# One layer of three attention groups on one core: how the rotary part of group B's scores is multiplied, and the order in which the out-projection begins

## The chip, the cores and the metric

The kernel runs on one core of a Trainium2 chip. The metric is the device time of one execution in microseconds (us), the median of several executions. TensorE (PE, with its weight loads PEld) multiplies; VectorE (DVE), ScalarE (ACT) and GpSimd (POOL) work beside it; SyncE (SP) and POOL issue the transfers.

## The reference

The layer computes, for 1024 tokens of width 2048 in float32:

```
h = RMSNorm(x);  proj = h @ W_in            # split among the groups
group A: 16 heads, 2 key heads, width 64, windows of 128 keys, sinks
group B: 4 heads; score = (q_nope . k_nope + q_rope . k_rope) * 192**-0.5
         q_nope 128 wide, q_rope 64 wide, k_rope shared by the heads
         mask: key chunk <= query chunk (chunks of 64); softmax; times v
group M: 4 heads of 128 over 256 memory tokens
y = x + [silu(gA)*A | silu(gB)*B | silu(gM)*M] @ W_o
```

`q_rope` and `k_rope` are RMS-normalised and rotated by the position. The output is y, 1024 x 2048.

## The kernel before

All stages use all five engines, each with its own instruction list written out by hand and semaphores between them. In order of time:

1. **In-projection** (to about 806 us). Weights stream from memory in chunks of 128x1024. Every float32 product is made of three fp32r matmuls (`three`, L1535): both operands are split into a high part (fp32r) and a low part (the rest), and hi\*hi, hi\*lo and lo\*hi are added in PSUM. ACT makes the high parts (`high`, L604), DVE the low ones (`low`, L935).
2. **Memory keys and values** (806 to 858 us, loop at L1607), in the same way. Beside it DVE normalises and rotates B's rotary key (`kr_d`, L1193 to L1198) and writes it twice side by side; TensorE transposes it (L1638), ACT keeps rows 0 to 63 in `krT[:, 0]` and rows 64 to 127 in `krT[:, 1]` (L744). The other half of each is zero (DVE, L1202). So a 128-row product with two heads' stacked queries picks one head.
3. **Up-projection of group B** (858 to about 940 us), eight token tiles. The step of a tile on TensorE is `up_in` (six transposes into PSUM banks 0 and 1), `up` (24 matmuls for queries, then 12 for keys and values) and `up_back` (transposes of the finished queries and keys of the tile two before: 2 rotary, 4+4 others). DVE squares, normalises and rotates (`up_squares`, `up_norm`), and makes the low part of the next tile's input (`up_in`, L1206). ACT keeps what is transposed (`up_keep`).
4. **Group A** (to about 1005 us), **group B** (to 1126 us) and **group M** (to 1165 us). Each is a pipeline of steps: scores on TensorE, maximum on DVE, exponent on ACT, normalisation on DVE, transposes on TensorE (`turn_p`), copy on ACT (`keep_pT`), values on TensorE, gating on DVE. On TensorE step s of group B is score(s+2), value(s-1), turn_p(s). A step is one head and one tile of 128 queries against 128 to 1024 keys; there are 32. A score of group B is, per 512 keys, one float32 matmul for the 128-wide part (L1719) and one for the rotary part (L1720). In the profile a float32 matmul is two instructions.
5. **Out-projection** (1165 us to the end): eight visits (pairs of output tiles) of eight units. Units 0 to 3 are the left half of the contraction in a seven-product scheme (Strassen-Winograd, products P1 to P7, 21 matmuls of 128x512), units 4 to 7 are plain (24 matmuls). The order within a visit is 0 to 7. In visit 0 ACT and DVE also split the gated attention results into high and low parts, unit by unit (`left_sums`, `left_high`, `left_low`, `plain_high`, `plain_low`), some of it beside group M (`ahead`). The weights of a unit come through three buffers `z` (SP), with sums by DVE (`z_make`), high part by ACT (`z_high`), low part by DVE (`z_low`). POOL loads x into `xq` and stores y from it.

The gates of the groups come by POOL's transfers into `mixed` (L562, L567, L572), which the gating multiplies in place. The probabilities of group B (`b_p`) lie at the start of the region of the raw weights.

Of the kernel before, what the change touches and what calls it, by code (L numbers as in the profile page):

```python
# [29 lines left out]
P = 128  # L30
# [40 lines left out]
NOUT = NVISIT * NUNIT  # L71
ZRING, HRING = 3, 2
# [54 lines left out]
def layer(nc, io):  # L127
    with ExitStack() as ctx:
# [46 lines left out]
        kr_d = at("kr_d", [P, TT, 2, BR], F32, R0 + 41984)  # L175
# [12 lines left out]
        qrT = at("qrT", [P, BH // 2, SEQ], F32, R0 + 49152)  # L188
        krT = at("krT", [P, 2, SEQ], F32, R0 + 57344)
# [47 lines left out]
        c_lo = put("c_lo", [P, 2, 6, P], F32R)  # L237
        u_tmp = at("u_tmp", [P, 2, 4, 32], F32, RS + 14336)
# [14 lines left out]
        b_p = at("b_p", [P, 2, SEQ], F32, WRAW)  # L253
# [13 lines left out]
        plain_at = [RT + 8192, RT + 12288] + [RS + 4096 * k for k in range(6)]  # L267
# [4 lines left out]
        zh_at = (R0 + 61440, small_at + 3584)  # L272
        z_hi = [at(f"z_hi{i}", [P, 7, P], F32R, zh_at[i]) for i in range(HRING)]
        xq = at("xq", [P, 4, HALF], F32, small_at + 7168)
        part_a = at("part_a", [P, HALF], F32, small_at + 15360)
        part_b = at("part_b", [P, HALF], F32, small_at + 17408)
        assert small_at + 19456 <= nc.sbuf_usable_end
# [61 lines left out]
        kn_loaded, kn_turned, kn_kept, zeroed = sem("kn_loaded"), sem("kn_turned"), sem("kn_kept"), sem("zeroed")  # L339
# [25 lines left out]
        def blocks_to(c):  # L365

            return NBLOCK * (c // NUNIT) + min(c % NUNIT, NBLOCK - 1) + 1

        def rotary_place(t):

            return (2, slice(0, 256)) if t < TT - 3 else (1, slice(256 * (t % 2), 256 * (t % 2) + 256))
# [3 lines left out]
        def _(sp):  # L375
# [83 lines left out]
            def load_z(c):  # L459
                wait(sp, z_used, c - ZRING + 1)  # L460
                if c % ZRING == 2:
                    sp.wait_ge(M.gated, TT)
                sp.dma_start(z[c % ZRING][:, 0:4, :], io["w_out"][c]).then_inc(z_loaded[c % ZRING], 16)
# [5 lines left out]
            for c in range(2, NOUT):  # L469
                load_z(c)  # L470


        @block.gpsimd
        def _(pool):
# [93 lines left out]
            for i in range(TT // 2):  # L568
# [3 lines left out]
                pool.dma_start(mixed[:, AJ + BH:KT, tok], gate_s[AJ + BH:KT, :, tok].rearrange("j p s -> p j s")  # L572
                               ).then_inc(M.gates_loaded, 16)

            def quad(a, visit, q):

                return a[2 * visit + q % 2, :, q // 2 * HALF:(q // 2 + 1) * HALF]

            pool.wait_ge(M.gated, TT)
            for visit in range(NVISIT + 1):  # L580
                for q in range(4):
                    if visit >= 1:
# [1391 lines left out]
```

## Time and profile before

| | us |
|---|---|
| median of 3 runs | 1513.98 (1510.68 to 1514.11) |
| the profiled execution, its own time | 1507.98 |
| its span | 1506.2 |
| PE busy | 1464.1 (97% of the span) |
| DVE busy | 671.9 (45%) |
| ACT busy | 469.2 (31%) |
| PE's share of the chain that ended last | 90% |

The granted clock of TensorE was 0.997 of full speed on average. The profile's first part gives the busy time of each engine; the chain of waits gives what each part of the end hung on. Because PE is busy nearly throughout, what counts is PE's own time, and in the few stretches where it idles, whom it waits for.

### The profile page before, as it was taken

Reading aid. Unit: us, or ns where it says so; the run is one execution under the profiler, and the core shown is the slowest. Engines: PE = TensorE matmul, PEld = TensorE weight load, DVE = VectorE, ACT = ScalarE, POOL = GpSimd, SP = SyncE. Lnnn points to the kernel's source line nnn. Section 1 sums busy time; section 2 is a strip of 40 time slices with the busy share of each in tenths; the row PEclk is TensorE's granted clock in tenths of the full one; section 3 lists DMA queues with packets and bytes.
Section 4 is the critical chain, followed back from the end, with each engine's and each line's share of the span. In section 5 each row is a group of like instructions: output and inputs, shape, how many; then the busy total and the mean of one; then the engine's idle time right before and its main releaser. Section 6 shows DMA issues by size and latency. Waiting matters only on the chain.

```text
span 1506.2 us, 17987 instructions
## 1 busy us (share of the span) xinstructions
PE 1464.1 (97%) x7118; PEld 1195.7 (79%) x7118; DVE 671.9 (45%) x1055; ACT 469.2 (31%) x842; POOL 130.6 (9%) x141
## 2 busy tenths in 40 slices
PE   9999999999999999999999998889998999999997
PEld 7888888888888888887887787656777788888886
DVE  4332241442614131312226767975659654444542
ACT  4551301313131020201234456974456411111110
POOL 1010000202001000000001022100000011111110
PEclk9999999999999999999999999999999999999999
DMA  9541231121123121221444521540020233333331
GB/s 359 196 107 56 98 111 55 42 101 52 42 102 108 57 97 56 81 72 43 167 154 155 181 84 42 155 127 15 15 71 17 75 112 106 105 112 105 108 109 49
DMA packets 48812, 146.78 MB, mean 97 GB/s; under 512 B 5616, under 2 KB 9712, under 8 KB 47472
## 3 DMA queue, kind: packets, MB, share of 16 engines
q1 hardware_dynamic: 33136, 84.42, 17.8%
q0 software_dynamic: 15472, 61.51, 11.7%
q8 instruction: 41, 0.67, 0.2%
q14 instruction: 19, 0.16, 0.0%
q10 hardware_dynamic: 144, 0.02, 0.0%
HBM read 117.61 MB, written 28.32 MB: 97 GB/s over the span
## 4 chain that ended last, share of the span: by engine, by line
PE 90%; ACT 5%; DVE 3%; issue 1%; DMA 0%; POOL 0%; ACTq 0%; SPq 0%; DVEq 0%
PE ps L1537 26%; PE ps L1539 26%; PE ps L1538 26%; ACT a_p L805 3%; PE ps L1756 2%; PE ps L1719 2%; PE ps L1720 2%; PE ps L1737 1%; PE ps L1723 1%; PE ps L1762 1%; PE ps L1591 0%; PE ps L1590 0%; DVE w_lo L938 0%; ACT st L803 0%; PE ps L1741 0%
## 5 line engine op out<-in xcount | busy, mean ns | idle before, releaser
L938 DVE TENSOR_TENSOR w_lo<-w_raw,w_hi 128x1024 fp32r<-128x1024 f32 x87 | 106.6, 1225 | 504.0 <-ACT w_hi L608 503.6
L608 ACT ACTIVATE w_hi<-w_raw 128x1024 fp32r<-128x1024 f32 x89 | 94.2, 1059 | 593.8 <-PE ps L1539 573.9
L1537 PE MATMUL ps<-w_hi,h_hi 128*128 128x512 f32 x640 | 249.5, 390 | 1.4 <-DVE h_lo L953 1.4
L1539 PE MATMUL ps<-w_hi,h_lo 128*128 128x512 f32 x640 | 249.4, 390 | 0.0
L1538 PE MATMUL ps<-w_lo,h_hi 128*128 128x512 f32 x640 | 249.3, 390 | 0.0
L1539 PE MATMUL ps<-h_hi,w_lo 128*128 128x512 f32 x512 | 199.5, 390 | 0.0
L1537 PE MATMUL ps<-h_hi,w_hi 128*128 128x512 f32 x512 | 199.5, 390 | 0.0
L1538 PE MATMUL ps<-h_lo,w_hi 128*128 128x512 f32 x512 | 199.5, 390 | 0.0
L1538 PE MATMUL ps<-mixed_lo,z_hi 128*128 128x512 f32 x384 | 149.6, 390 | 0.0
L1537 PEld LDWEIGHTS ps<-w_hi,h_hi 128*128 128x128 f32 x640 | 120.2, 188 | 26.5 <-issue 1.6
L1539 PEld LDWEIGHTS ps<-w_hi,h_lo 128*128 128x128 f32 x640 | 120.2, 188 | 24.9
L1538 PEld LDWEIGHTS ps<-w_lo,h_hi 128*128 128x128 f32 x640 | 120.2, 188 | 24.9
L883 ACT ACTIVATE z_hi<-z 128x896 fp32r<-128x896 f32 (+1 forms) x64 | 50.7, 792 | 255.3 <-PE ps L1539 203.4
L1430 DVE TENSOR_TENSOR z_lo<-z,z_hi 128x896 fp32r<-128x896 f32 (+1 forms) x64 | 57.1, 892 | 130.6 <-ACT z_hi L883 130.6
L1537 PEld LDWEIGHTS ps<-h_hi,w_hi 128*128 128x128 f32 x512 | 96.1, 188 | 20.1
L1539 PEld LDWEIGHTS ps<-h_hi,w_lo 128*128 128x128 f32 x512 | 96.1, 188 | 19.9
L1538 PEld LDWEIGHTS ps<-h_lo,w_hi 128*128 128x128 f32 x512 | 96.1, 188 | 19.8
L1539 PE MATMUL ps<-plain_hi,z_lo 128*128 128x512 f32 x256 | 99.7, 390 | 0.0
L1537 PE MATMUL ps<-plain_hi,z_hi 128*128 128x512 f32 x256 | 99.7, 390 | 0.0
L1537 PE MATMUL ps<-left_hi,z_hi 128*128 128x512 f32 x224 | 87.6, 391 | 4.2 <-DVE left_slo L1407 2.1
L1539 PE MATMUL ps<-left_hi,z_lo 128*128 128x512 f32 x224 | 87.3, 390 | 0.0
L1538 PEld LDWEIGHTS ps<-mixed_lo,z_hi 128*128 128x128 f32 x384 | 72.1, 188 | 14.9
(270 smaller groups left out, 2090.9 us busy)
## 6 DMA issues: line engine op xcount, KB each, us to landing
w_raw<-in_w SPq DMA_DIRECT2D x89, 512.0 KB, 3.5
z<-in_w_out SPq DMA_DIRECT2D x64, 256.0 KB, 2.7
x_nat<-in_x POOLq DMA_DIRECT2D x8, 1024.0 KB, 8.6
mixed<-gate_s POOLq DMA_DIRECT2D x16, 512.0 KB, 4.9
xq<-in_xT POOLq DMA_DIRECT2D x32, 256.0 KB, 4.5
out_y<-xq POOLq DMA_DIRECT2D x32, 256.0 KB, 2.6
x_raw<-in_xT SPq DMA_DIRECT2D x7, 1024.0 KB, 18.2
gate_s<-T POOLq DMA_DIRECT2D x3, 2048.0 KB, 7.0
```

Of the source, the lines that this page charges most:

```text
L608: a.activation(w_hi[:, n % SPLIT, :], w_raw[:, n % RAW, :], ACT.Copy).then_inc(hi_ready, 1)
L805: ins = a.activation(a_p[:, par, e, :], ps[:, 2 + 2 * par + e // 4, e % 4 * P:(e % 4 + 1) * P], ACT.Exp, bias=st[:, par, 1, e:e + 1], scal ...
L883: a.activation(flat(z_hi[c % HRING][:, 0:n, :]), flat(z[c % ZRING][:, 0:n, :]), ACT.Copy).then_inc(z_hi_made, 1)
L938: v.tensor_tensor(w_lo[:, n % SPLIT, :], w_raw[:, n % RAW, :], w_hi[:, n % SPLIT, :].bitcast(F32), ALU.subtract).then_inc(lo_ready, 1)
L1430: v.tensor_tensor(flat(z_lo[c % ZRING][:, 0:n, :]), flat(z[c % ZRING][:, 0:n, :]), flat(z_hi[c % HRING][:, 0:n, :]).bitcast(F32), ALU.subt ...
L1537: mm(out, a_hi, b_hi, start=start, stop=False)
L1538: mm(out, a_hi, b_lo, start=False, stop=False)
L1539: return mm(out, a_lo, b_hi, start=False, stop=stop)
L1719: mm(out, qnT[:, h, q], knT[:, h, a:b], start=True, stop=False)
L1720: ins = mm(out, qrT[:, h // 2, q], krT[:, h % 2, a:b], start=False, stop=True)
L1723: ins = mm(ps[:, bank + h // 2, h % 2 * NMEM:(h % 2 + 1) * NMEM], c_qT[:, par, h, :], kmT[:, h, :], start=True, stop=True)
L1756: ins = mm(ps[:, 1, 0:P], vB[:, k, h * BV:(h + 1) * BV], b_pT[:, par, k * P:(k + 1) * P], start=(k == 0), stop=(k == t))
```

## The change

Rotary part of group B:

- The rotary query of a head is stored stacked: 64 rows of high part (fp32r) over 64 rows of low part, instead of two heads stacked in float32. DVE makes both after the rotation (`u_r`, two more operations in a tile). There are four 128-column transposes of a tile for it in place of two, in two groups: heads 0 and 1 where the two transposes stood, heads 2 and 3 between the two halves of `up` two tiles later (for the first five tiles), and in `up_back` for the last three. The second group waits until DVE has made the low part of the next tile's input, because both use PSUM bank 1. ACT copies each group by itself.
- The rotary key is kept twice: `kr_high` is high over high, `kr_low` is low over zero. With the stacked query, the first product gives (q_hi + q_lo) * k_hi and the second q_hi * k_lo. 16 transposes in place of 8; the two clearing operations on `krT` go, one smaller one comes.
- A score is then two fp32r matmuls (at least 256 keys wide, so some columns are computed and not used) and one float32 matmul.
- `b_p` moves into the rows of `mixed` that hold the gates of M's heads 0 and 1, so these gates are loaded only after B's last transpose, by one transfer of 1 MB, for which M's gating waits (`late_gates`).

Out-projection:

- The units of a visit go in the order 0, 1, 4, 2, 5, 3, 6, 7, and the weights are loaded in that order.
- The products P1, P5 and P7, P2 and P3 of the first unit are issued between the last steps of group M, P4 before M's last gating, and only P6 waits for it.
- The work beside M is laid out anew: weights of units 0 and 1 are finished there, the left operand of unit 2 later. Sums that leave PSUM are taken at unit positions 6 and 7 of every visit.
- Loads of x and stores of y move from POOL to SP, behind the weight loads of positions 2, 3 and 4.

```diff
+ORDER = (0, 1, 4, 2, 5, 3, 6, 7)
-        b_p = at("b_p", [P, 2, SEQ], F32, WRAW)
+        b_p = at("b_p", [P, 2, SEQ], F32, R1 + 49152)
@@ SP
+            def load_xq(visit):
+                for q in range(4):
+                    wait(sp, xq_moved[q], 32 * visit)
+                    sp.dma_start(xq[:, q, :], quad(io["xT"], visit, q)).then_inc(xq_moved[q], 16)
+            def store_y(visit):
+                for q in range(4):
+                    sp.wait_ge(drained, 9 * visit + 6 + q)
+                    sp.dma_start(quad(io["yT"], visit, q), xq[:, q, :]).then_inc(xq_moved[q], 16)
...
             for c in range(2, NOUT):
                 load_z(c)
+                if c == 2:
+                    load_xq(0)
+                if c >= NUNIT and c % NUNIT == 3:
+                    store_y(c // NUNIT - 1)
+                if c >= NUNIT and c % NUNIT == 4:
+                    load_xq(c // NUNIT)
@@ POOL
+            pool.wait_ge(B.p_turned, len(BSTEPS))
+            pool.dma_start(mixed[:, AJ + BH:AJ + BH + 2, :], gate_s[...]).then_inc(late_gates, 16)
@@ ACT
+            def keep_qr(t, i, bank, col):
+                act.wait_ge(u_qr, 2 * t + 2 - i)
+                a.activation(qr[i][:, :, t * P:(t + 1) * P],
+                             ps[:, bank, col:col + 256].rearrange("p (h s) -> p h s", h=2), ACT.Copy).then_inc(u_qr_kept, 1)
...
-                if 2 <= c <= 5:
-                    left_high(1 + (c - 2) // 2, c % 2)
-                if c == 6:
-                    z_high(0)
+                if c in (2, 3):
+                    left_high(1, c - 2)
+                if c in (4, 5):
+                    z_high(c - 4)
+                if c in (6, 7):
+                    left_high(2, c - 6)
+                    plain_high(c + 2)
@@ DVE
-            v.tensor_copy(kr_d[:, :, 1:2, :], kr_d[:, :, 0:1, :]).then_inc(kr_norm, 1)
+            steps.did(v.memset(kr_l0[:, :, 1, :].bitcast(F32), 0.0))
+            steps.did(v.tensor_copy(kr_hh[:, :, 0, :], kr_d[:, :, 0, :]))
+            do(v.tensor_copy(kr_hh[:, :, 1, :], kr_d[:, :, 0, :]))
+            v.tensor_tensor(kr_l0[:, :, 0, :], kr_d[:, :, 0, :], kr_hh[:, :, 0, :].bitcast(F32), ALU.subtract).then_inc(kr_norm, 1)
             low(n + 1)
-            for g in range(2):
-                rows = slice(64 - 64 * g, 128 - 64 * g)
-                v.memset(krT[rows, g, :], 0.0).then_inc(zeroed, 1)
...
-                v.tensor_tensor(d2, d2, u_tmp[:, 1], ALU.add).then_inc(u_done, 1)
+                do(v.tensor_tensor(d2, d2, u_tmp[:, 1], ALU.add))
+                do(v.tensor_copy(u_r[:, t % 2, :, 0, :], rope(u_fin)))
+                v.tensor_tensor(u_r[:, t % 2, :, 1, :], rope(u_fin), u_r[:, t % 2, :, 0, :].bitcast(F32), ALU.subtract
+                                ).then_inc(u_done, 1)
...
+                if at_ is M:
+                    dve.wait_ge(late_gates, 16)
...
+                if c in (0, 1):
+                    left_sums(1, c)
+                if c in (2, 3):
+                    z_make(c - 2)
+                if c in (5, 6):
+                    z_low(c - 5)
+                if c in (4, 5):
+                    left_sums(2, c - 4)
+                if c in (6, 7):
+                    left_low(1, c - 6)
@@ PE
+                if 0 <= t - 2 < SPLIT_TILES:            # in up(t), between queries and keys
+                    turn_qr(t - 2, 1, 1, 256)
...
+            def turn_qr(t, i, bank, col):
+                pe.wait_ge(u_done, t + 1)
+                if i == 1:
+                    pe.wait_ge(u_clo, min(t + 4, TT))
+                for h in range(2 * i, 2 * i + 2):
+                    ins = turn(ps[:, bank, col + (h - 2 * i) * P:col + (h - 2 * i + 1) * P],
+                               u_r[:, t % 2, h].rearrange("p a d -> p (a d)").bitcast(F32), ident[:])
+                if t < SPLIT_TILES or i == 1:
+                    ins.then_inc(u_qr, 1)
...
-                        mm(out, qnT[:, h, q], knT[:, h, a:b], start=True, stop=False)
-                        ins = mm(out, qrT[:, h // 2, q], krT[:, h % 2, a:b], start=False, stop=True)
+                        wide = max(b, a + 256)
+                        for kr, start in ((kr_high, True), (kr_low, False)):
+                            mm(ps[:, bank + a // HALF, 0:wide - a], qr[h // 2][:, h % 2, q], kr[:, a:wide], start=start, stop=False)
+                        ins = mm(out, qnT[:, h, q], knT[:, h, a:b], start=False, stop=True)
...
+            def out_begun(part):
+                if part == 0:
+                    pe.wait_ge(z_lo_made, 1)
+                    pe.wait_ge(left_lo_made, 2)
+                    pe.wait_ge(M.qT, TT)
+                    product(0, P1)
+                elif part == 1:
+                    pe.wait_ge(M.exp, TT)
+                    product(0, P5)
+                    product(0, P7)
+                else:
+                    product(0, P2)
+                    product(0, P3)
```

## Rows read from the trace of the kernel before

**Rows 1.** The page, part 1: busy time, share of the span, instructions.

```profile
PE 1464.1 (97%) x7118; PEld 1195.7 (79%) x7118; DVE 671.9 (45%) x1055; ACT 469.2 (31%) x842; POOL 130.6 (9%) x141
```

**Rows 2.** Stretches: length, busy PE, PEld, DVE, ACT, POOL, PEclk, DMA share, GB/s.

```profile
857.00:925.00 68.00, 67.79 (x398) 59.10 (x397) 43.96 (x97) 34.94 (x50) 16.60 (x8) 1.00 0.22 66
925.00:998.00 73.00, 60.04 (x585) 44.27 (x583) 65.56 (x142) 69.08 (x294) 10.44 (x11) 0.98 0.52 143
1060.00:1111.00 51.00, 50.41 (x269) 35.57 (x269) 28.62 (x88) 19.24 (x43) 1.51 (x2) 1.00 0.06 22
1126.00:1165.00 39.00, 33.39 (x250) 30.66 (x249) 35.63 (x50) 28.04 (x65) 0.00 (x0) 1.00 0.10 33
1165.00:1205.00 40.00, 35.85 (x155) 29.06 (x156) 27.56 (x39) 16.51 (x18) 2.15 (x4) 1.00 0.25 73
```

**Rows 3.** Timeline of PE in group B: start, length, instruction.

```profile
1101.58 0.60 PE L1720 MATMUL ps<-krT,qrT 128*128 128x256 f32 x2
1102.01 0.83 PE L1756 MATMUL ps<-b_pT,vB 128*128 128x128 f32 x6
...
1103.12 1.02 PE L1719 MATMUL ps<-knT,qnT 128*128 128x512 f32 x2
1103.98 1.02 PE L1720 MATMUL ps<-krT,qrT 128*128 128x512 f32 x2
```

**Rows 4.** Timeline of PE in the up-projection: fp32r matmuls of 512 and 256 columns.

```profile
869.56 0.39 PE L1539 MATMUL ps<-uq_hi,c_lo 128*128 128x512 f32 x1
869.79 0.28 PE L1537 MATMUL ps<-uq_hi,c_hi 128*128 128x256 f32 x1
869.90 0.28 PE L1538 MATMUL ps<-uq_lo,c_hi 128*128 128x256 f32 x1
```

**Rows 5.** Timeline of group B where one head ends and the next begins.

```profile
1085.15 1.60 PE L1756 MATMUL ps<-b_pT,vB 128*128 128x128 f32 x12 [0.45 <-ACT b_pT L824]
...
1087.55 0.92 ACT L824 ACTIVATE b_pT<-ps 128x896 f32<-128x896 f32 x1 [1.36 <-PE ps L1737]
...
1088.52 1.83 PE L1756 MATMUL ps<-b_pT,vB 128*128 128x128 f32 x14
```

**Rows 6.** Timeline of the up-projection, one tile: transposes, DVE's low part, key matmuls.

```profile
881.54 0.38 PE L1674 MATMUL ps<-ident,u_fin 128*128 128x128 f32 x2
881.76 0.60 PE L1678 MATMUL ps<-ident,u_fin 128*128 128x128 f32 x4
...
887.39 0.95 DVE L1206 TENSOR_TENSOR c_lo<-ps,c_hi 128x768 fp32r<-128x768 f32 x1
...
887.52 0.40 PE L1537 MATMUL ps<-ukv_hi,c_hi 128*128 128x512 f32 x1
```

**Rows 7.** Timeline of the memory stage: a clearing operation, and PE's longest wait.

```profile
834.82 0.91 DVE L1202 MEMSET krT<- 64x1024 f32 x1 [0.27 <-PE ps L1539]
...
839.70 0.50 PE L1537 MATMUL ps<-w_hi,m_hi 128*128 128x512 f32 x1 [2.07 <-DVE w_lo L938]
```

**Rows 8.** Timeline at the start of group A: the last tile's rotary query.

```profile
938.38 0.44 PE L1674 MATMUL ps<-ident,u_fin 128*128 128x128 f32 x2 [2.19 <-DVE u_fin L1268]
...
938.86 0.38 ACT L772 ACTIVATE qrT<-ps 128x256 f32<-128x256 f32 x1
```

**Rows 9.** Timeline of group M and the first matmul of the out-projection.

```profile
1122.23 0.75 POOL L572 DMA_DIRECT2D mixed<-gate_s  x1 [30.26 <-DVE mixed L1305]
...
1131.06 0.69 DVE L1305 TENSOR_TENSOR mixed<-ps,mixed 128x512 f32<-128x512 f32 x1 [0.40 <-PE ps L1762]
...
1165.74 0.50 PE L1537 MATMUL ps<-left_hi,z_hi 128*128 128x512 f32 x1 [0.78 <-DVE mixed L1305]
```

**Rows 10.** DMA issues: what, queue, count, KB each, median us to landing.

```profile
z<-in_w_out SPq DMA_DIRECT2D x64, 256.0 KB, 2.7
x_nat<-in_x POOLq DMA_DIRECT2D x8, 1024.0 KB, 8.6
mixed<-gate_s POOLq DMA_DIRECT2D x16, 512.0 KB, 4.9
xq<-in_xT POOLq DMA_DIRECT2D x32, 256.0 KB, 4.5
out_y<-xq POOLq DMA_DIRECT2D x32, 256.0 KB, 2.6
```

More of the change, by code:

```diff
@@ L365, in blocks_to, with unit, qr_steps @@
         def blocks_to(c):
-            return NBLOCK * (c // NUNIT) + min(c % NUNIT, NBLOCK - 1) + 1
-        def rotary_place(t):
-            return (2, slice(0, 256)) if t < TT - 3 else (1, slice(256 * (t % 2), 256 * (t % 2) + 256))
+            return NBLOCK * (c // NUNIT) + sum(u < NBLOCK for u in ORDER[:c % NUNIT + 1])
+        def unit(c):
+            return ORDER[c % NUNIT]
+        SPLIT_TILES = TT - 3
+        def qr_steps(t):
+            return t + min(t, SPLIT_TILES)
         @block.sync
@@ L470, in _ @@
                 load_z(c)
+                if c == 2:
[4 more added lines that the diff above has]
+                    load_xq(c // NUNIT)
+            store_y(NVISIT - 1)
+            for q in range(4):
+                sp.wait_ge(xq_moved[q], 32 * NVISIT)
         @block.gpsimd
@@ L1663, in up @@
                 ins.then_inc(u_up, 1)
+            def turn_qr(t, i, bank, col):
[7 more added lines that the diff above has]
+                    ins.then_inc(u_qr, 1)
             def up_back(t):
-                bank, cols = rotary_place(t)
-                rotary = ps[:, bank, cols]
                 fin = u_fin[:, t % 2]
-                pe.wait_ge(u_done, t + 1)
-                wait(pe, u_qr_kept, t)
+                wait(pe, u_qr_kept, qr_steps(t))
                 wait(pe, u_q_out, min(t + 3, TT))
-                for h in range(2):
-                    ins = turn(rotary[:, h * P:(h + 1) * P], fin[:, h * P:(h + 1) * P], ident[:])
-                ins.then_inc(u_qr, 1)
+                if t < SPLIT_TILES:
+                    turn_qr(t, 0, 2, 0)
+                else:
+                    turn_qr(t, 0, 1, 0)
+                    turn_qr(t, 1, 1, 256)
                 wait(pe, u_qn_kept, t)
@@ L1774, in begin, with tiles_of @@
                     turn_q(at_, k % 2)
-            def tiles_of(at_, n, before=None, after=None):
+            def tiles_of(at_, n, before=None, after=None, beside=None):
                 def body(i):
@@ L1780, in body @@
                         c = i * 2 + par
+                        if beside and c == n - 1:
+                            beside(1)
                         if below(c + 2, n):
```

171 lines of the change are left out of this document (90 added, 81 removed).

## The prediction

> **What bounds the kernel now.** I read the busy times first, then a table of stretches, then the timeline of each stretch that the change touches. PE is busy 1464.1 us of the span of 1506.2 [rows 1], so a microsecond of PE work taken off counts in full, unless PE waits there for another. The stretches [rows 2] say where that is. In the up-projection PE idles 0.2 us of 68 and in group B 0.6 of 51, with DVE and ACT at little over half: PE bounds both. In group A ACT is busy 69.08 of 73 and PE 60.04: ACT bounds it, and a late start moves all of it. In group M DVE is busy 35.63 of 39 and PE idles 5.6; in visit 0 of the out-projection PE idles 4.2 of 40. From there to the last output PE runs dense, and the change leaves the number of matmuls there as it is.
>
> **Group B's scores.** A float32 matmul of 512 columns takes 1103.98 - 1103.12 = 0.86 us from start to start, one of 256 columns 1102.01 - 1101.58 = 0.43 [rows 3], so 0.215 for 128 columns. A head has tiles of 1 to 8 times 128 keys, 36 in all; four heads make 144 x 0.215 = 31.0 us for the rotary part. It is replaced by pairs of fp32r matmuls. One of 512 columns takes 869.79 - 869.56 = 0.23, one of 256 takes 0.11 to 0.12 [rows 4], one of 384 between them 0.17. A pair is then 0.46, 0.23, 0.34. The eight tiles of a head take 0.23 + 0.23 (128 keys are computed as 256) + 0.34 + 0.46 + 0.69 + 0.69 + 0.80 + 0.92 = 4.36; four heads 17.4. PE work falls by 13.6 us.
>
> Some of this cannot be collected. Value(s) waits for ACT's copy of step s's transposes, and score(s+3) is what covers it. At a head's end the long copies meet the short scores of the next head: the copy of 896 columns starts at 1087.55, lasts 0.92, and value starts at 1088.52, right when it ends [rows 5]. The score in between, 256 keys, falls from 0.86 to 0.66: that 0.2 is given back. One step later the copy is about 0.1 longer and the score (384 keys) falls from 1.29 to 0.99: 0.3 given back. One step earlier PE waits already (0.45) and the 128-key score is no shorter. 0.5 us for each of three head ends, 1.5 in all; at worst DVE's order (maximum before gate before normalisation) adds as much again. Elsewhere DVE has 22 us of slack in 51. I take -12, bounds -13.6 and -10.
>
> **Transposes.** Two take 881.76 - 881.54 = 0.22 [rows 6]. Two more in each of eight tiles and eight for the key are 24 x 0.11 = 2.6 us, in stretches that PE bounds: +2.6.
>
> **A new wait in the up-projection.** The transposes of heads 2 and 3 stand between the query and the key matmuls of `up`, and wait for DVE's low part of the tile just brought in. In the trace the key matmuls start at 887.52, but that low part starts at 887.39 and takes 0.95, to 888.34 [rows 6]. So PE, which did not wait here, will wait about 0.9 us with the signal. Behind it on PE stand the twelve key matmuls, for which ACT and in turn DVE's next low part wait: the loop closes, so this is lost in every tile and not made up. Five tiles have it (the first a little less, as DVE doesn't yet keep keys): 5 x 0.9 = 4.4 us. Bounds: 0, if DVE comes earlier relative to PE; 7, if the loop lengthens by the copy too. DVE's two added operations (some 0.3 and 0.4 by its 128x128 and 128x256 operations) fall into its wait for ACT and cost nothing there.
>
> **Start of group A.** For the last tile nothing covers them: PE waits 2.19 us for the rotated query, and ACT's copy follows at 938.86 [rows 8], on the engine that bounds A. DVE +0.75, two transposes 0.22, one copy more 0.3: +1.3; bounds 0.5 and 2.
>
> **Memory stage.** Two clearing operations of 0.91 go, and with them their place ahead of the low part for which PE waits 2.07 us [rows 7]. What comes instead (a memset, two copies, one subtraction on 128x512, by my estimate some 2 us, against the 1.8 and one copy removed) stands earlier, where DVE otherwise waits for ACT. The wait should mostly vanish; then the next chunk is just in time, or late on its own transfer. I take -1.5; bounds -2.1 and +0.5.
>
> **Group M and visit 0.** The first unit is 21 matmuls, about 4.8 us. Before, it starts at 1165.74, on the last gating [rows 9]. Now all but P6 fills PE's idle time in M's last steps; P6 follows the last gating, near the same time, and takes 0.7. That is -4.1. The later waits in visit 0 (3.4 of the 4.2 us idle [rows 2]) don't go. Following the lists with the durations above, I find unit 2's weights 0.3 late, then unit 5's 2.4 late (its high part stands behind both `left_high` of unit 3 on ACT, which wait for DVE's sums), and unit 3's 1.5 late: 4.2 us. Sum -4; bounds -8 (all covered) and 0.
>
> The late gates: POOL issues at 1122.23 the transfer after which this one comes [rows 9], so it leaves at about 1123.8 of that timeline; M's first gating is at 1131.06, 7.3 us later. A transfer of 1 MB took 8.6, of 512 KB 4.9 [rows 10]; between them, with twice the size of the latter, I expect it 0 to 1.3 us late, on a DVE that has some slack of its own by then: +0.3; bounds 0 and 2.
>
> The Trainium skill ("DMA: Bandwidth & Descriptors", "Anatomy of one DMA") gives 2.0 us plus bytes over 436 GB/s for such a transfer, which would be 4.4 us for 1 MB, and nothing is then late. The trace does not bear the rule out for this kind of transfer: 512 KB would be 3.2 us by it and took 4.9 [rows 10].
>
> x and y over SP in place of POOL: the same 256 KB land in 2.7 us on SP, 4.5 and 2.6 on POOL [rows 10], and SP waits for each unit anyway. At the very end it may save a part of an issue: 0, bounds -1 and +0.5.
>
> **Sum.** -12 + 2.6 + 4.4 + 1.3 - 1.5 - 4 + 0.3 = -8.9 us. The profiled execution took 1507.98 (span 1506.2 and 1.8 around it) and would take 1499.1. The median shown is 1513.98, 6 us above it, so the forecast for the median is 1505.1. A difference of 0.3% (4.5 us) is about what a measurement here can tell from none.
>
> **Rivals.**
> (a) *The new wait closes into a longer loop, and B gives back more at head ends.* For it: DVE's list in the up-projection is serial with ACT's (squares, keep, low part), and the copy of heads 2 and 3 is a new link on ACT. Against: ACT is busy 34.94 of 68 [rows 2]. With the wait at 7, B at -10 and the rest as above: -4.3, time 1509.7, no measurable change.
> (b) *The wait in the up-projection doesn't come, and the stalls of visit 0 go too.* For it: 0.9 us is a small lag, visit 0 has the same work in a more even order. Against: the chain from the last key matmul through ACT to DVE's low part is the same in each tile. -13.3 to -17: time 1497 to 1500.7, say 1499.
> (c) *Each fp32r matmul in B shows its weight load (slower than before).* Place: group B, where two fp32r and two float32 passes alternate on short columns and each loads its weights anew. A weight load is 1195.7 / 7118 = 0.17 us on average [rows 1]. Four heads have 48 column groups, 96 fp32r matmuls; fully exposed they cost 16 us, and the sum becomes +7, time 1521. It decides from 0.09 us exposed per matmul, where the gain of 8.9 is gone. Against it: two matmuls of 256 columns start 0.11 apart [rows 4], less than one load, so loads hide behind matmuls even there; only the change between the two kinds of matmul isn't shown by a row.
> The Trainium skill ("TensorE: Matmul & The Clock Gate", Part 3) says that a weight load overlaps a running matmul only when the row groups differ; that would be (c) in full. The trace disagrees, since all these use all 128 rows and still start 0.11 apart [rows 4].
> (d) *The change does nothing for B, because another bounds it at once.* DVE 28.62 and ACT 19.24 of 51 [rows 2] speak against it. The sum without B's 12 is +3.1: time 1517; with a third of B's gain it is no change.
>
> **From this the numbers.** Forecast (between -5 and -12): 0.64. (a) 0.15, (b) 0.14, (c) 0.03, (d) 0.04. Faster by over 0.3%: the forecast, (b) and a third of (a), 0.83; within 0.3%: the rest of (a) and half of (d), 0.12; slower: (c) and the other half of (d), 0.05. The range reaches from (b) to beyond (a) with the scatter of the runs (3.4 us): 1497 to 1512.
>
> **What would show it.** Group B: PE busy between A's end and the last B transposes about 12 us less, pairs of fp32r starts 0.23 apart at 512 columns, the float32 part unchanged at 0.86, and waits for `b_pT` at head ends of about 0.3 more. Up-projection: a wait of PE before L1206's product in five tiles of about 0.9, a tile's period of 8.7 grown to about 9.8 us. Memory stage: the wait of 2.07 gone. First matmul of the out-projection before M's last values; unit 0 done about 0.7 after the last gating; PE waits of about 4 us in visit 0. Wrong if the up-projection's period stays, if B's stretch shrinks by less than 10 us, or if M's first gating waits for the late gates by more than 2 us.

## The result, and the profile after

| | before | after |
|---|---|---|
| median | 1513.58 (4 runs, 1510.68 to 1514.11) | 1495.70 (4 runs, 1495.27 to 1497.86) |
| the profiled execution, its own time | 1507.98 | 1495.54 |
| its span | 1506.2 | 1493.7 |

The ratio is 0.9889, 95% interval 0.9871 to 0.9906. The change saves 16.8 us by the ratio, where I forecast 8.9; the time lies 1.3 us below the range. The direction was right, the size was not.

The page of the kernel after, part 1, stands against [rows 1]: PE is busy 7.8 us less in a span that is 12.4 us shorter (1506.20 and 1493.75). So part of the gain isn't work that PE no longer does.

```profile
PE 1456.3 (97%) x7142; PEld 1196.8 (80%) x7142; DVE 675.8 (45%) x1072; ACT 472.0 (32%) x850; POOL 97.6 (7%) x78
```

To see where the time went I took six marks in each trace, starts or ends of DVE instructions that both kernels have, and the end of the span, and compared the stretches between them. A gating's mark is its start, the last sum's its end. The forecast beside it is my prediction's terms for the same stretch.

```
stretch, us                                          before   after    diff  forecast
start to the first low part of the up-projection     856.56   855.67   -0.9   -0.6
to A's first gating (up-projection, start of A)       90.32    98.98   +8.7   +7.5
to A's last gating                                    61.19    61.68   +0.5    0
to B's last gating (group B)                         118.16   106.71  -11.5  -12
to M's last gating (group M)                          38.77    38.54   -0.2   +0.3
to the last sum of the output (out-projection)       332.17   329.65   -2.5   -4
to the end of the span                                 9.03     2.52   -6.5    0
sum                                                  1506.20  1493.75  -12.4   -8.9
```

(In the forecast's column, the transposes' 2.6 are split 0.9 and 1.7, and the sum's small difference is rounding.)

**Group B.** The timeline of the kernel after shows the score of one step against seven key tiles (512 and 384 columns), to be held against [rows 3], the same step of the kernel before.

```profile
1100.31 0.83 PE L1819 MATMUL ps<-b_pT,vB 128*128 128x128 f32 x6
1100.98 0.60 PE L1800 MATMUL ps<-ident,b_p 128*128 128x128 f32 x4
1101.34 0.48 PE L1782 MATMUL ps<-kr_high,qr 128*128 128x512 f32 x1
1101.65 0.39 PE L1782 MATMUL ps<-kr_low,qr 128*128 128x512 f32 x1
1101.89 1.02 PE L1783 MATMUL ps<-knT,qnT 128*128 128x512 f32 x2
...
1103.73 1.05 PE L1819 MATMUL ps<-b_pT,vB 128*128 128x128 f32 x8
```

The first fp32r matmul starts 0.31 us before the second, the second 0.24 before the float32 one. The cost of a pair is better read from the whole step, because the score now also starts 0.08 us sooner behind its transposes. From the values of one step to those of the next it is 1103.73 - 1100.31 = 3.42 us. Before it was 4.12: the values of [rows 3] start at 1102.01, the next ones here (kernel before):

```profile
1106.13 1.05 PE L1756 MATMUL ps<-b_pT,vB 128*128 128x128 f32 x8
```

The 0.70 us less are what pairs of 0.46 and 0.34 us in place of float32 matmuls of 0.86 and 0.645 give.

At a head's end PE now waits 0.34 us where it did not in [rows 5] (1088.52), and one step later value starts 0.29 us after the last score's 0.64 us are over, just when ACT's copy of 1024 columns is done (1090.94 + 1.02):

```profile
1087.23 0.92 ACT L855 ACTIVATE b_pT<-ps 128x896 f32<-128x896 f32 x1 [1.36 <-PE ps L1800]
1088.20 1.83 PE L1819 MATMUL ps<-b_pT,vB 128*128 128x128 f32 x14 [0.34 <-ACT b_pT L855]
...
1090.94 1.02 ACT L855 ACTIVATE b_pT<-ps 128x1024 f32<-128x1024 f32 x1 [2.44 <-PE ps L1800]
1091.09 0.81 PE L1783 MATMUL ps<-knT,qnT 128*128 128x384 f32 x2
1092.02 2.05 PE L1819 MATMUL ps<-b_pT,vB 128*128 128x128 f32 x16
```

**Up-projection and start of A.** PE's waits of the kernel after, from 857 to 932 us (engine, line, whom it waits for; us in total, times, longest), and below them the timeline of one tile against [rows 6]: the transposes of heads 2 and 3 wait for the low part that starts at 878.05.

```profile
PE ps L1722 <- DVE c_lo L1243: 4.4, 5, 1.1
PE ps L1581 <- ACT S L754: 0.2, 1, 0.2
```

```profile
878.05 0.95 DVE L1243 TENSOR_TENSOR c_lo<-ps,c_hi 128x768 fp32r<-128x768 f32 x1
879.15 0.41 PE L1722 MATMUL ps<-ident,u_r 128*128 128x128 f32 x2 [1.13 <-DVE c_lo L1243]
```

At the start of A, against [rows 8], the wait for the last tile's rotary query has grown from 2.19 to 3.54. Behind it the same matmuls take almost twice as long for some time: 2.08 us for sixteen at 947.06, 1.20 at 951.78. The timeline of the kernel after:

```profile
944.20 0.63 PE L1722 MATMUL ps<-ident,u_r 128*128 128x128 f32 x4 [3.54 <-DVE u_r L1307]
944.66 0.65 PE L1739 MATMUL ps<-ident,u_fin 128*128 128x128 f32 x4
945.11 1.06 PE L1743 MATMUL ps<-ident,u_fin 128*128 128x128 f32 x4
947.06 2.08 PE L1771 MATMUL ps<-a_kT,a_qT 64*128 64x128 f32 x16 [0.89 <-issue]
...
951.78 1.20 PE L1771 MATMUL ps<-a_kT,a_qT 64*128 64x128 f32 x16
```

**Memory stage.** The two rows of the kernel after answer to [rows 7]: the memset takes 0.48 and the wait of 2.07 is gone, 0.2 is left.

```profile
831.29 0.48 DVE L1235 MEMSET kr_l<- 128x512 f32 x1
837.56 0.50 PE L1581 MATMUL ps<-w_hi,m_hi 128*128 128x512 f32 x1 [0.23 <-DVE w_lo L975]
```

**Out-projection.** Visit 0 of the kernel after: PE waits three times for the low part of a unit's weights, 4.6 us in all.

```profile
1174.69 0.50 PE L1581 MATMUL ps<-left_hi,z_hi 128*128 128x512 f32 x1 [1.18 <-DVE z_lo L1472]
1181.91 0.50 PE L1581 MATMUL ps<-plain_hi,z_hi 128*128 128x512 f32 x1 [2.12 <-DVE z_lo L1472]
1188.95 0.50 PE L1581 MATMUL ps<-left_hi,z_hi 128*128 128x512 f32 x1 [1.26 <-DVE z_lo L1472]
```

M's first gating waits 0.40 us for PE at 1127.87 and for no transfer, so the late gates are in time. Their transfer was issued at 1119.76 and took 6.7 us.

**The end.** This is the term that I put at zero. What the DMA engines moved from 1490 to 1510 us, in 40 slices of half a microsecond (busy tenths, GB/s), first of the kernel before, then of the one after:

```profile
DMA  0000000008539067084000000000000000000000
GB/s 0 0 0 0 0 0 0 0 0 336 189 123 385 17 246 279 0 344 180 0 0 0 0 0 0 0 0 0 0 0 0 0 0 0 0 0 0 0 0 0
```

```profile
DMA  1580850000000000000000000000000000000000
GB/s 45 209 315 0 307 217 0 0 0 0 0 0 0 0 0 0 0 0 0 0 0 0 0 0 0 0 0 0 0 0 0 0 0 0 0 0 0 0 0 0
```

Before, the last byte moves in the 19th slice, that is before 1499.5, and the span ends at 1506.2: 6.7 us in which nothing is moved and no engine is busy. After, the last byte moves in the 6th slice, before 1493.0, and the span ends at 1493.7. The timelines have the last issues of both; nothing comes behind them:

```profile
1496.48 0.69 DVE L1501 TENSOR_TENSOR xq<-ps,xq 128x512 f32<-128x512 f32 x1 [0.67 <-PE ps L1539]
1497.46 0.54 POOL L584 DMA_DIRECT2D out_y<-xq  x1 [0.82 <-DVE xq L1501]
```

```profile
1487.28 4.31 SPq L489 DMA_DIRECT2D out_y<-xq  x4
1490.54 0.69 DVE L1544 TENSOR_TENSOR xq<-ps,xq 128x512 f32<-128x512 f32 x1 [0.67 <-PE ps L1583]
```

### The profile page after: what moved, and what is told of

Read it like the earlier page. It is cut to its first block, busy times and chain, and to the rows that moved or that the text cites. A ratio compares the mean times of both kernels' runs of the same rounds, so it can differ in the third digit from the quotient of the medians.

```text
span 1493.7 us, 18069 instructions
## 1 busy us (share of the span) xinstructions
PE 1456.3 (97%) x7142; PEld 1196.8 (80%) x7142; DVE 675.8 (45%) x1072; ACT 472.0 (32%) x850; POOL 97.6 (7%) x78
## 4 chain that ended last, share of the span: by engine, by line
PE 86%; ACT 6%; DVE 5%; issue 2%; DMA 1%; POOL 0%; ACTq 0%; SPq 0%; DVEq 0%
PE ps L1581 25%; PE ps L1583 25%; PE ps L1582 25%; ACT a_p L836 2%; PE ps L1819 2%; PE ps L1783 2%; PE ps L1800 1%; PE ps L1782 1%; PE ps L1786 1%; DVE ss L1280 1%; ACT u_fin L795 1%; PE ps L1635 1%; PE ps L1634 0%; PE ps L1825 0%; ACT b_pT L855 0%
## 5 line engine op out<-in xcount | busy, mean ns | idle before, releaser
L914 ACT ACTIVATE z_hi<-z 128x512 fp32r<-128x512 f32 (+1 forms) x64 | 50.6, 791 | 253.8 <-PE ps L1583 208.5
L1472 DVE TENSOR_TENSOR z_lo<-z,z_hi 128x512 fp32r<-128x512 f32 (+1 forms) x64 | 57.0, 891 | 140.6 <-ACT z_hi L914 140.6
```

Source lines behind the costliest of these rows:

```text
L914: a.activation(flat(z_hi[c % HRING][:, 0:n, :]), flat(z[c % ZRING][:, 0:n, :]), ACT.Copy).then_inc(z_hi_made, 1)
L1472: v.tensor_tensor(flat(z_lo[c % ZRING][:, 0:n, :]), flat(z[c % ZRING][:, 0:n, :]), flat(z_hi[c % HRING][:, 0:n, :]).bitcast(F32), ALU.subt ...
```

## The experiments

Two things were open: whether the end is what it seems, and why the median of the kernel before lies 5.6 us above its profiled execution while the median of the kernel after does not. Twelve kernels ran, four at a time, each four on one chip with runs of the kernel before beside them (medians 1512.04, 1512.42 and 1512.72).

**e1, the kernel before once more.** No edit.

> The kernel before, once more, with a profile of its own. The profiled execution of the kernel before took 1507.98 us, but the median of its runs is 1513.6, 5.6 us more; the kernel after has its profile at its median (1495.5). Theory: executions of the kernel before differ by about 3 to 6 us among themselves, and a second profile, if it is nearer to 1513, shows the extra in one place: at the end, between the last DVE instruction and the end of the span (9.0 us in the first profile), or at the starts of POOL's transfers. Rival: the profile's execution is about 5 us shorter by way of its being profiled, then this one gives 1508 again and the end is again 9.0.

Measured: 1513.83 (1511.31 to 1515.02), ratio 1.0008 (0.9999 to 1.0018), its profiled execution 1514.13. The end is again 9.0, so the theory's first place was wrong; its rival was too. The extra is elsewhere. Of 58 executions of this kernel beside the first profile, none is below 1510.15: the execution on which I built was an unusually fast one. The marks say where the 6.1 us are: 1.5 before the up-projection, 1.4 up to A's first gating, 0.8 in A, 2.5 in M (41.23 in place of 38.77), nothing behind that. The granted clock is down at 7 to 12 us, at 932 to 947 us (but for 937 to 939) and at 1161 to 1169 us, that is in the first, second and last of these places; the 0.8 us in A follow right behind the second, between A's first and second gating (4.75 in place of 3.95 us). The stretches around the start of A and the end of M follow (length, busy PE, PEld, DVE, ACT, POOL, granted clock, DMA share, GB/s), in the first profile of the kernel before and then in this one. The first profile isn't free of it either: its clock is 0.50 from 931 to 934 us.

```profile
925.00:955.00 30.00, 23.31 (x227) 18.56 (x226) 26.26 (x61) 26.08 (x102) 5.82 (x5) 0.94 0.52 137
1155.00:1172.00 17.00, 12.44 (x75) 10.62 (x76) 14.69 (x22) 5.14 (x9) 2.15 (x4) 1.00 0.25 76
```

```profile
925.00:955.00 30.00, 24.34 (x203) 20.09 (x201) 24.23 (x55) 23.53 (x87) 5.39 (x5) 0.83 0.44 121
1155.00:1172.00 17.00, 11.13 (x68) 9.87 (x67) 13.37 (x19) 7.46 (x15) 0.00 (x0) 0.80 0.01 1
```

In slices of 2.5 us the clock in e1 is 0.50, half of full speed (1.2 for 2.4 GHz), from 1162.5 to 1167.5. The timeline of e1 shows what PE did before and what the clock cost: after two waits sixteen matmuls take 3.78 us that took 2.05 before and after.

```profile
1160.24 1.09 PE L1741 MATMUL ps<-ident,c_p 128*128 128x128 f32 x8 [1.75 <-DVE c_p L1364]
1162.45 3.78 PE L1762 MATMUL ps<-c_pT,vM 128*128 128x128 f32 x16 [1.11 <-ACT c_pT L824]
1169.05 2.05 PE L1762 MATMUL ps<-c_pT,vM 128*128 128x128 f32 x16 [1.11 <-ACT c_pT L824]
```

**e2, the kernel before with x and y over SP.** The edit, in SP's list and with POOL's loop taken out:

```diff
             for c in range(2, NOUT):
                 load_z(c)
+                if c == 2:
+                    load_xq(0)
+                if c >= NUNIT and c % NUNIT == 3:
+                    store_y(c // NUNIT - 1)
+                if c >= NUNIT and c % NUNIT == 4:
+                    load_xq(c // NUNIT)
+            store_y(NVISIT - 1)
```

> The kernel before with only one edit: the loads of x and the stores of y are issued by SP behind the same weight loads as in the kernel after. Theory (the end of the program is the term that I mis-sized): the 9.0 us between the last DVE instruction and the end of the span become about 2.5, and the time falls by 6.5, ratio 0.9957; if the scatter of the kernel before also comes from POOL's transfers, by up to 12, ratio 0.992. Rival (the gain comes from the out-projection's order or from group B alone): the end stays at 9.0 or what it saves is lost in visits, change under 1 us, ratio 0.9993 to 1.000.

Measured: 1507.53 (1505.04 to 1511.31), ratio 0.9966 (0.9945 to 0.9987), 5.1 us. The last sum ends at 1503.21 and the span at 1505.7: an end of 2.5. The other stretches are those of e1, dips included (M 41.22). The theory of the end holds, with 6.5 us forecast and an interval of 2.0 to 8.3. The scatter isn't POOL's: the runs still spread over 6 us.

**e3, the kernel after with x and y given back to POOL.** The reverse of e2's edit.

> The kernel after with x and y given back to POOL, all else as it is. Theory of the end: slower by about 6.5 us, 1502.2 us, with 9.0 us between the last DVE instruction and the end of the span; up to 12 slower if POOL's transfers also make the executions scatter. Rival: under 1 us, 1496.5 us at most.

Measured: 1502.37 (1501.08 to 1502.84), ratio to before 0.9932 (0.9916 to 0.9949). Against the 0.9889 of the change this is 0.0043, or 6.5 us. Its last sum ends at 1491.17, that of the kernel after at 1491.23; its end is 9.1. The whole difference is in the end.

**e4, the kernel before with only the last four stores over SP.**

```diff
-                    if visit >= 1:
+                    if 1 <= visit < NVISIT:
                         pool.wait_ge(drained, 9 * (visit - 1) + 6 + q)
@@ SP, at the end
+            for q in range(4):
+                sp.wait_ge(drained, 9 * (NVISIT - 1) + 6 + q)
+                sp.dma_start(<y of the last visit, q>, xq[:, q, :]).then_inc(y_last, 16)
+            sp.wait_ge(y_last, 64)
```

> The kernel before, where only the four stores of the last visit, and the wait for them, are on SP; the 28 stores and 32 loads before them stay on POOL. Theory that the last transfer's queue sets the end: as with all of them on SP, 6.5 us less, ratio 0.9957, and the end at about 2.5 us. Rival, that it is the use of POOL's queue during the last visits, or its load on the visits, which costs: no gain here, under 1 us.

Measured: 1506.08 (1502.62 to 1507.59), ratio 0.9962 (0.9948 to 0.9976), 5.7 us, with an end of 2.4. So the 60 transfers before the last four don't account for the gain; 5.1 and 5.7 us aren't told apart.

**e5, POOL sends, SP waits.** The last wait for `xq_moved` moves from POOL's list to SP's.

> The kernel before; all stores of y still go out by POOL, but the last wait for them is on SP, and POOL's list ends with the issue of the last store. Moving the last four stores to SP gave about 6 us (end 9.0 to 2.4 us). Theory 1, the cost belongs to POOL's way of sending (it has to be wound up after its last transfer): the end stays at 9.0 us, time as before, 1512. Theory 2, the cost belongs to the wait on POOL's list (POOL is slow to see that the store has landed and to end): the end falls to about 2.7, time 1506.

Measured: 1510.62 (1509.36 to 1515.27), ratio 0.9992 (0.9982 to 1.0003). The last sum ends at 1500.78 and the span at 1507.8: an end of 7.0. The last issue of its timeline, and its transfers in slices of half a microsecond from 1495 us:

```profile
1501.07 0.54 POOL L586 DMA_DIRECT2D out_y<-xq  x1 [0.82 <-DVE xq L1501]
```

```profile
GB/s 0 0 0 0 0 0 246 279 57 385 82 156 369 0 254 270 0 0 0 0 0 0 0 0 0 0 0 0 0 0 0 0 0 0 0 0 0 0 0 0
```

The last byte moves before 1503.0, 4.8 us before the end, though nobody on POOL waits for it. By this profile both theories have a share: 2.0 us of the 6.5 are POOL's wait, 4.5 come with a transfer that POOL has issued, whoever waits. It is one profile, and the times (1.2 us by the ratio) don't tell the 2.0 from nothing; that the greater part stays is shown by both. What happens in these 4.5 us no row shows.

**e6, the rotary part alone**, with the out-projection of before, and **e7, the out-projection's part alone**. Each takes its half of the diff that stands above.

> The rotary part of the change alone (scores of B, the two extra operations and transposes in the up-projection, the late gates), with the out-projection of the kernel before. From the stretches of the two profiles: memory stage -0.9, up-projection +6.7, start and course of A +2.4, B -11.4, M 0: -3.2 us, ratio 0.998, about 1509, with the end still at 9.0 us. Rival, that the rotary part is the main gain, as my prediction had it (-12 + 2.6 + 4.4 + 1.3 - 1.5 + 0.3 = -4.9, with no more said of it), gives 1507; the rival that nearly all is the out-projection: 0 or slower.

> The out-projection's part of the change alone (order of units, products begun beside M, x and y by SP), with the rotary scores of the kernel before. From the profiles: visit 0 -3.2 (M's last value to the first finish), later visits +0.6, end -6.5: -9.1 us. And a second profile of the kernel before had TensorE at half clock at 1160 to 1170, where M ends and PE idles, for about 2.5 us of time; with products placed there PE doesn't idle and this is gone in every execution: down to -11.6, so ratio 0.9925 to 0.994. Rival, that the dip of the clock stays or comes elsewhere: -9.1 at most, ratio 0.994 or more.

Measured: e6 1504.73 (1504.19 to 1507.52), ratio 0.9956 (0.9941 to 0.9972), 6.7 us; e7 1500.88 (1499.00 to 1501.95), ratio 0.9931 (0.9915 to 0.9948), 10.4 us. Together 17.1, the change as a whole 16.8: the halves add. For e6 both numbers of mine were too small (the interval is 4.2 to 8.9 us, so it leaves out the 3.2 and still holds the rival's 4.9). Its profile differs from the first profile of before as foreseen (-3.6 us of span; 98.95 in the up-projection and start of A, 106.67 for B with its start), but its median is at its profile, that of before is not: its profile has no dip at the end of M (38.81), and four of its five executions have a mean clock of 0.996. Why this half should be spared the dip I don't know; M's code is the same in it. e7 came out as the theory says, 10.4 between 9.1 and 11.6, with M at 38.52, though the 0.6 that it adds for later visits isn't there (see the point on visit 0 below). A shorter dip shows at 1186 to 1190 us, behind the wait of 2.13 in visit 0.

**e8, the second group of rotary transposes later.** In the kernel after:

```diff
-                if 0 <= t - 2 < SPLIT_TILES:
-                    turn_qr(t - 2, 1, 1, 256)
                 wait(pe, u_kv_out, 2 * t)
                 for k in range(2):
+                    if k == 1 and 0 <= t - 2 < SPLIT_TILES:
+                        turn_qr(t - 2, 1, 1, 256)
```

> The kernel after, with the transposes of heads 2 and 3 in the up-projection moved from before the twelve key matmuls to between their two halves of six (1.4 us later). Theory: the wait of PE for DVE's low part (4.4 us in five tiles, 0.8 to 1.1 each) goes: -4.4 us, ratio 0.997, about 1491. Rival, that the period of a tile is now set by DVE and ACT (9.97 us), with the wait moving to another instruction: 0 to -1.

Measured: 1490.58 (1489.67 to 1492.44), ratio to before 0.9859 (0.9842 to 0.9875). That is 5.1 us below the kernel after by the medians, which were taken on different chips, and 4.5 us by the ratios, each to the kernel before on its own chip. PE's only wait from 857 to 927 us is the one of 0.2:

```profile
PE ps L1581 <- ACT S L754: 0.2, 1, 0.2
```

The wait was all loss, as the prediction had it, and needed only 1.4 us of other work in front of it. A tile's period, from one low part to the next, is 8.73 us in the kernel before, 9.97 in the one after and 8.96 here. The profiled execution, 1492.44, is the slowest of the four, with the clock at 0.50 from 939 to 952 us.

**e9, the kernel before with PE's idle stretches filled.** The positions in M's last steps are those of `out_begun`:

```diff
+            for k in range(2):                          # before scores_ready(A, 0)
+                mm(ps[:, 3, :], krT[:, 0, 0:P], krT[:, 0, 0:HALF], start=True, stop=True)
@@ up_back, t == TT - 1, before the wait for u_done
+                    for k in range(2):
+                        mm(ps[:, 1, :], krT[:, 0, 0:P], krT[:, 0, 0:HALF], start=True, stop=True)
@@ M's last steps, parts 0, 1 and 2
+                for bank in ((0, 0), (2, 3, 2), (4, 5, 4))[part]:
+                    mm(ps[:, bank, 0:NMEM], kmT[:, 0, 0:P], kmT[:, 0, :], start=True, stop=True)
```

> The kernel before with matmuls added that compute nothing used, where TensorE idles: two of 512 columns (0.86 us each) before group A's first scores, two before the rotary transposes of the last tile, and eight of 256 columns (0.43 each) in M's last steps, at the places where the kernel after puts the first products of the out-projection. Theory: executions of the kernel before scatter and are slower than its first profile because the granted clock falls to half after these idle stretches (930 to 950 us, 1155 to 1170 us in two further profiles, costing 6 us together). With the stretches filled the clock stays at 1.00 there: 2 to 5 us faster though 6.9 us of work was added, ratio 0.997 to 0.9985, and no granted clock under 1.00 at 1155 to 1170. Rival: the clock has other causes, the dips stay, and the added work shows where it doesn't fit the idle time: 0 to +3 us.

Measured: 1509.96 (1507.21 to 1512.10, 11 runs), ratio 0.9980 (0.9971 to 0.9989): 3 us faster with 6.9 us of work added. The mean clock of its executions is 0.996 to 0.998, that of the ten of e1 was 0.990 to 0.994. From the first low part to A's first gating it takes 89.45 us (90.32 in the first profile of the kernel before, 91.75 in e1), from B's last gating to M's last 38.78 (38.77 and 41.23), so the added work fits the idle time. The same two stretches as above:

```profile
925.00:955.00 30.00, 25.90 (x239) 18.71 (x237) 26.55 (x63) 27.16 (x106) 5.82 (x5) 1.00 0.54 141
1155.00:1172.00 17.00, 15.59 (x92) 13.44 (x93) 14.39 (x22) 5.16 (x5) 2.15 (x4) 1.00 0.31 91
```

**e10, e8 with fill at the start of A.** Seven fp32r matmuls of 512 columns before A's first scores, eleven before the last tile's rotary transposes, on `kr_high`.

> The kernel after with the late transposes (as e8) and fill matmuls only at group A's start: seven fp32r of 512 columns (0.23 each) before A's first scores and eleven before the last tile's rotary transposes, in PE's waits of 1.94 and 3.07 us. Theory: the half clock of 930 to 955 us in e8's profile (5.3 us of clock lost) goes, A's first gating comes at about 951 instead of 953.3, and the time falls by 1.5 to 3 us against e8's 1490.6, to about 1488.5. Rival: A is bound by ACT alone and PE's clock at its start doesn't matter: within 0.7 us of 1490.6; or the clock falls before the fill and the fill itself runs at half speed: 1 to 3 us slower.

Measured: 1487.59 (1486.15 to 1487.80), ratio 0.9836 (0.9821 to 0.9851), 3.0 us below e8 by the medians and 3.5 by the ratios. Both intervals are wide enough to overlap, but the slowest run here, 1487.80, is below the fastest of e8, 1489.67. The stretch at the start of A in e8 and in e10:

```profile
925.00:955.00 30.00, 24.10 (x182) 20.57 (x182) 22.90 (x54) 20.97 (x73) 4.93 (x4) 0.72 0.42 112
```

```profile
925.00:955.00 30.00, 26.24 (x248) 20.48 (x246) 27.31 (x63) 26.45 (x103) 5.82 (x5) 1.00 0.50 136
```

In the first, ACT, which bounds A, is busy 20.97 us, in the second 26.45: beside a PE at half clock it gets less to do. The stretch from the first low part of the up-projection to A's first gating is 97.12 in e8 and 91.79 here. The timeline of e10 shows the fill and what is left of the wait:

```profile
934.72 2.81 PE L1734 MATMUL ps<-kr_high 128*128 128x512 f32 x11
938.31 0.65 PE L1722 MATMUL ps<-ident,u_r 128*128 128x128 f32 x4 [0.78 <-DVE u_r L1307]
```

**e11, a second move in the kernel of e8**, and **e12, all together**.

```diff
-                if c == 2:
-                    left_high(3, 0)
-                    left_high(3, 1)
+                if c in (2, 3):
+                    left_high(3, c - 2)
```

> The kernel after with the late transposes (as e8) and one more move: ACT's high part of the second sum for unit 3 comes after the weights of the fifth position, not before. In the profile of the kernel after, PE waits 2.12 us at 1181.9 for the low part of unit 5's weights, whose high part stands behind this on ACT. Theory: that wait falls by ACT's 0.6 to 1.1 us and the next by none: 1 us faster than e8, about 1489.6. Rival: the wait moves to unit 3 (its own sums come later): 0.

> The two moves and the fill matmuls together. Theory, if both count and add: 1.5 to 3 from the fill and 1 from the second move, against e8's 1490.6: 1487 to 1488, ratio to the kernel before 0.983. Rival, none of them counts: 1490.6.

Measured: e11 1490.14 (1488.50 to 1490.57), ratio 0.9850 (0.9835 to 0.9865); e12 1487.45 (1485.86 to 1489.93), ratio 0.9831 (0.9815 to 0.9846). The second move isn't told apart from nothing by the times. The waits say why: the one for unit 5's weights falls from 2.1 to 0.8, but a new one of 0.74 stands before it, and from M's last gating to the last sum e11 takes 327.82 us, e8 328.40. On one chip with each other, e12 is 2.7 us below e11, which differs from it by the fill alone: a second measure of what the fill gives. It doesn't rule out every dip. In the profile of e12, 1489.93 and its slowest run, PE waits 2.03 us at 953 us for a load of group A's queries, and the clock is 0.50 from 956 to 961 us; A takes 63.77 us where e10 has 61.23:

```profile
955.43 1.16 PE L1773 MATMUL ps<-a_kT,a_qT 64*128 64x128 f32 x16 [2.03 <-DMA a_q_at<-aq_s]
```

PE's waits from 1160 to 1215 us, e8 first, then e11:

```profile
PE ps L1581 <- DVE z_lo L1472: 3.4, 2, 2.1
```

```profile
PE ps L1580 <- DVE z_lo L1471: 2.8, 3, 1.3
```

e10 and e12 are the fastest kernels measured, some 25 us below the kernel before and 8 below the one after.

## Why the prediction was wrong, point by point

**The step that failed** is the term for x and y: "At the very end it may save a part of an issue: 0, bounds -1 and +0.5". It measures -6.5, four ways: 6.5 between the first two traces, 6.5 between the change and e3, an end of 2.5 for 9.0 in e2, 2.4 in e4. Only the last four of the 64 transfers count (e4). I had weighed the landing times in [rows 10], 2.7 against 2.6, which are alike indeed: the last four stores land in 2.3 us by POOL and 2.0 by SP. What I hadn't looked at is the time behind the landing. Two rows would have told me: a last issue by POOL at 1497.46, landing after 2.6 us, and a span of 1506.2.

**The base failed as well.** "The profiled execution ... would take 1499.1. The median shown is 1513.98, 6 us above it, so the forecast for the median is 1505.1." This took the 6 us for something that any kernel carries. In the one further profile of the kernel before they lie at stretches of lowered clock (e1), filling two of these gives 3 us back (e9), and the kernel after loses less: its profile is at its median. This is worth 16.8 - 12.4 = 4.4 us of the gain. How much of it comes from M's end alone stays open, as e6 is spared the dip there too. Of the six profiles in which M's end is as before and not filled (before, e1, e2, e4, e5, e6) three show the dip there (e1, e2, e5), for 2.5 us each; of the seven with products of the out-projection in M's last steps (after, e3, e7, e8, e10, e11, e12) none does. That filling the stretch removes it is shown for both stretches together (e9) and for the start of A by itself (e10); for the end of M alone it was not tried.

Against the profile the other terms come to -5.9 where they were to be -8.9. So the account is -8.9 + 3.0 (the other terms) - 6.5 (the end) - 4.4 (the base) = -16.8. None of the three signs of being wrong came: the up-projection's period grew (8.73 to 9.97 for 8.7 to 9.8), B's stretch shrank by 11.5, M's first gating waited for no gates. The mechanisms named were right, and what decided was not among them. That the time missed the range by only 1.3 us is luck, for the 3.0 stand against the other two errors. Term by term:

- *Group B, -12, bounds -13.6 and -10.* Measured -11.5. The size of the matmuls was right (a pair 0.46 and 0.34, by the whole step). Given back were 2.1 us of the 13.6 and not 1.6, at the head ends and one step behind, by ACT's copy as worked out; the wait for `b_pT` is 2.0 in all against 1.4.
- *Transposes +2.6, new wait +4.4.* The wait measured 4.4 in five tiles, longest 1.13, to the tenth; e8 confirms that nothing makes it up. The closed loop of rival (a) would have shown as a longer wait and didn't.
- *Start of A, +1.3.* With the line above, this was to be 7.5 and is 8.7. The missing 1.2 lies behind the last tile's low part: from there to A's first gating it is 33.31 us before and 36.74 after. I put it down to the clock, at 0.50 from 945.5 to 951.5 us after a wait of 3.54 us: in e8, with a longer dip, the same stretch is 39.17, in e10, with the fill and no dip, 33.81. The clock was nowhere in the prediction's term, which had only what DVE, PE and ACT do more.
- *Memory stage, -1.5.* The wait of 2.07 went; with the transposes the stretch gained 0.9 for 0.6.
- *Group M and visit 0, -4; later visits 0.* Measured -2.5, all of it in visit 0: from M's last gating to the first matmul of visit 1 it is 45.68 us before and 43.16 after, and each of the six visits behind that which can be timed from first matmul to first matmul takes 40.80 in both kernels. P6 alone follows the last gating, and M isn't longer for the products put into it. The wait of 2.12 for unit 5's weights came as worked out (2.4), so did one behind it (1.26 for 1.5). The one for unit 2's weights was 1.18 for 0.3, and most of the shortfall is this: ACT's high part of the weights one position earlier (`z_high`, at 1166.24) begins 3.9 us after their load is issued, in e3, e7, e8 and e10 2.6 to 2.7 us, and DVE's list, where unit 2's weights come later, is held up with it. In those four the wait is 0.2 or less and visit 0 gains 3.5 to 3.8, near the 4 forecast; so in the profile of the kernel after this part comes from one slow load, and not from the order (e12's shows the same, 3.7 us and a wait of 0.96). (The first sum of the output can't mark the visits: in the new order it comes 1.1 us earlier in its visit.)

```profile
1166.24 0.63 ACT L914 ACTIVATE z_hi<-z 128x512 fp32r<-128x512 f32 x1 [4.49 <-DMA z<-in_w_out]
```

```profile
1163.12 0.63 ACT L914 ACTIVATE z_hi<-z 128x512 fp32r<-128x512 f32 x1 [3.23 <-DMA z<-in_w_out]
```

(The first row is of the kernel after, the load issued at 1162.30; the second of e8, issued at 1160.44.)

- *Late gates, +0.3.* Nothing was late. 1 MB took 6.7 us, inside the 7.3 worked out and the 8.1 from its issue to M's first gating. The rule of the Trainium skill that I had set against it ("DMA: Bandwidth & Descriptors", "Anatomy of one DMA") gave 4.4 for it; the trace decides for 6.7, and the conclusion is the same by both.
- *Rival (c), exposed weight loads.* Fell. The first fp32r matmul behind the transposes starts 0.31 before the next where 0.23 is its own time, but it starts 0.03 us after the last transpose does where the float32 one started 0.11 after it, so it is no loss; the second of a pair takes 0.24, at 384 columns 0.17, at 256 columns 0.12. *Rival (d)* fell with B.

## What to carry to other kernels

Look at the very end of a profile, at the time from the last byte moved to the end of the span: here it was 6.7 us with a last store issued by POOL and 0.7 with one by SP, and four moved stores gave it back. A profile is one execution; before its time is the base of a sum, hold it against the whole spread of runs, and look for stretches where the granted clock is down. Here the clock was halved in some executions after PE had waited 1 to 3.5 us on another engine or a load, so useful work, or even useless matmuls, put there was worth more than its own time. When stretches are compared by a mark, the mark must stand at the same point of the work in both kernels.

## What the runs showed of the hardware

- The time after the last transfer. With POOL's stores 9.0 to 9.1 us pass from the last sum to the end (five profiles), with SP's 2.5 (eight profiles, 2.45 to 2.52). With POOL's store and SP's wait it is 7.0 (e5).
- The granted clock fell to 0.50 where PE had waited 1.75 and 1.11 us (e1), 1.94 and 3.07 (e8), 3.54 (after), 2.13 (e7), 2.09 (e4), 2.03 (e12), and stayed there for 3 to 14 us. The same waits were followed by a full clock elsewhere: the first profile of the kernel before, with waits of 1.74 and 1.11, had 1.00 at M's end, and e8, with one of 2.14 in visit 0, 1.00 behind it. In e10, with no wait over 1 us at the start of A, no slice of 5 us before the last has less than 1.00.
- A float32 matmul of 512 columns takes 0.86 us from start to start, an fp32r one 0.23. Switching between them costs nothing that can be seen: a whole step takes 3.42 us, 0.70 less than before, as these times give.
